# A one-core chain of three transformer blocks: the first two weight tiles after four norms taken together by TensorE

## The reference

```
hn = rmsnorm(h, norm_w)
proj = hn @ w_in
```

## Time and profile before

| what | value |
|---|---|
| median of 3 runs | 4354.56 us (4347.96 to 4360.67) |
| the profiled execution | 4353.11 us, span 4351.3 us |
| mean granted PE clock | 0.931 of full |
| PE busy | 3978.3 us, 91% |
| DVE busy | 2144.5 us, 49% |
| ACT busy | 917.8 us, 21% |
| POOL busy | 1042.5 us, 24% |
| chain that ended last, by engine | PE 82%, DVE 11%, ACT 3%, DMA 2%, issue 2%, POOL 1% |

### The profile page before, as it was taken

One profiled execution on the slowest core, in us unless ns is written; L12 is line 12 of the kernel. 1 busy time (PEld: TensorE's weight loads), 2 busy tenths in 40 slices (PEclk: granted clock), 3 DMA queues, 4 the chain that ended last, 5 costly groups with the idle time before them and its releaser, 6 DMA issues.

```text
span 4351.3 us, 49214 instructions
## 1 busy us (share of the span) xinstructions
PE 3978.3 (91%) x19946; PEld 3238.7 (74%) x19946; DVE 2144.5 (49%) x2770; ACT 917.8 (21%) x1652; POOL 1042.5 (24%) x581
## 2 busy tenths in 40 slices
PE   7899998999999999999898996799989698889898
PEld 6677676788888888788776684677778577777777
DVE  3454546332333344999334433443335984753554
ACT  2434334200000032111011001302211112531031
POOL 1120220334434422333211120021222231003221
PEclk9999999999999998999999997797999897879999
DMA  1000000111121110222211111020473134212111
GB/s 74 25 30 16 30 30 16 63 63 58 64 66 58 63 34 30 83 87 82 73 41 47 49 55 66 25 72 20 134 109 79 58 103 131 66 51 77 63 44 58
DMA packets 139196, 260.31 MB, mean 60 GB/s; under 512 B 45584, under 2 KB 87568, under 8 KB 135952
## 3 DMA queue, kind: packets, MB, share of 16 engines
q1 hardware_dynamic: 72208, 156.26, 12.3%
q10 hardware_dynamic: 66816, 101.63, 6.9%
HBM read 209.35 MB, written 46.14 MB: 59 GB/s over the span
## 4 chain that ended last, share of the span: by engine, by line
PE 82%; DVE 11%; ACT 3%; DMA 2%; issue 2%; POOL 1%; ACTq 0%; SPq 0%; DVEq 0%; POOLq 0%
PE bank L543 22%; PE bank L544 21%; PE bank L545 21%; PE bank L650 4%; PE bank L779 2%; PE bank L912 2%; PE bank L742 1%; PE bank L1041 1%; PE bank L901 1%; PE bank L762 1%; DVE hn L1738 1%; DVE fb L1876 1%; DVE xl L1749 1%; DVE s5t L2206 1%; DVE pb L2205 1%
## 5 line engine op out<-in xcount | busy, mean ns | idle before, releaser
L543 PE MATMUL bank<-xh,wh 128*128 128x512 f32 x3008 | 1201.2, 399 | 118.8 <-ACT xc L1550 39.1
L544 PE MATMUL bank<-xl,wh 128*128 128x512 f32 x3008 | 1183.8, 394 | 0.0
L545 PE MATMUL bank<-xh,wl 128*128 128x512 f32 x3008 | 1182.4, 393 | 0.0
L500 POOL CAST wh<-raw 128x1024 fp32r<-128x1024 f32 x264 | 282.9, 1072 | 3196.7 <-PE bank L545 3142.6
L543 PEld LDWEIGHTS bank<-xh,wh 128*128 128x128 f32 x3008 | 573.1, 191 | 280.0 <-issue 85.4
L502 POOL TENSOR_TENSOR wl<-raw,wh 128x1024 fp32r<-128x1024 f32 x264 | 673.0, 2549 | 21.1
L545 PEld LDWEIGHTS bank<-xh,wl 128*128 128x128 f32 x3008 | 572.2, 190 | 122.2
L544 PEld LDWEIGHTS bank<-xl,wh 128*128 128x128 f32 x3008 | 573.3, 191 | 114.1
L2015 DVE SCALAR_TENSOR_TENSOR bank<-apad,cols,bank 128x512 f32<-128x512 f32 x406 | 267.9, 746 | 0.0
L1785 DVE TENSOR_TENSOR h<-bank,h 128x512 f32<-128x512 f32 x240 | 165.9, 691 | 183.9 <-PE bank L545 183.1
L1876 DVE TENSOR_TENSOR_SCAN fb<-fb 128x256 f32<-128x256 f32 (+7 forms) x128 | 186.4, 1497 | 106.3 <-ACT ab L1228 106.3
(11 more groups left out here) (331 smaller groups left out, 5488.1 us busy)
## 6 DMA issues: line engine op xcount, KB each, us to landing
raw<-in_wstream SPq DMA_DIRECT2D x264, 512.0 KB, 3.5
spills<-spill ACTq DMA_DIRECT2D x40, 512.0 KB, 2.7
rawm<-in_mod_w ACTq DMA_DIRECT2D x12, 1024.0 KB, 4.9
gate_spill<-gates ACTq DMA_DIRECT2D x16, 512.0 KB, 2.6
tabs<-in_rope ACTq DMA_DIRECT2D x4, 2048.0 KB, 8.2
f<-spills SPq DMA_DIRECT2D x8, 1024.0 KB, 5.8
h<-in_x ACTq DMA_DIRECT2D x4, 1024.0 KB, 11.9
tabs<-gate_spill ACTq DMA_DIRECT2D x4, 1024.0 KB, 7.2
```

The source lines that it names most:

```text
L500: nc.gpsimd.tensor_copy(wh[:, slot], raw[:, slot]).then_inc(S("panel_high"), 1)
L543: nc.tensor.matmul(o, lh, rh, start=start, stop=False)
L544: nc.tensor.matmul(o, lh, rl, start=False, stop=False)
L545: return nc.tensor.matmul(o, ll, rh, start=False, stop=stop)
```

## The change

PE takes the first two tiles after each of the four norms together in a new function `first_pair`: in each half, step s multiplies feature tile s for tile 0 into bank 0 and feature tile s-2 for tile 1 into bank 1. The units are renumbered: 0 and 1 are the first half of tile 0 and of tile 1, 2 and 3 the second half (before: 0 and 1 were the two halves of tile 0). The engines that take them out go by the new numbers; their places in the lists of ACT and DVE behind the norm stay. The first two panels' slots are free after 3 and 4 units in place of 2 and 4.

```diff
+PAIR_LAG = 2
+FIRST_FREED = [3, 4]
+
+
+def pair_unit(m, th, paired=True):
+
+    return 2 * th + m if paired else 2 * m + th
...
     start = [key for name in ("q0", "k0", "v0") for key in project(name)]
+    start[:4] = [start[n] for n in (0, 2, 1, 3)]
+    unit_of.update({key: n for n, key in enumerate(start)})
+    freed[:2] = FIRST_FREED
...
-                    split(panels(name, i) + m, before[m] if m < 2 else units(name, i) + PANEL_UNITS[name][m - 2])
+                    split(panels(name, i) + m, before[m] if m < 2 else units(name, i) + freed_after(name, i, m - 2))
...
+            def freed_after(name, i, m):
+
+                if i is None and m < 2 and name in ("ffn_first", "conv", "s5_u"):
+                    return FIRST_FREED[m]
+                return PANEL_UNITS[name][m]
...
-                        turn(name, i, [units(name, i) + (PANEL_UNITS[name][dp - 2 + m] - UNITS[name])
+                        last = None if i == 1 else i - 1
+                        turn(name, i, [units(name, i) + (freed_after(name, last, dp - 2 + m) - UNITS[name])
                                        for m in range(2)])
...
+            def first_pair(unit, panel, norm):
+
+                split_done(panel + 1)
+                slots = [(panel.b + m) % 2 for m in range(2)]
+                for th in range(2):
+                    t = slice(th * HALF, (th + 1) * HALF)
+                    for step in range(KT + PAIR_LAG):
+                        if step < KT:
+                            pe.wait_ge(S("norm_low"), SPLIT0[norm] + th * KT + step + 1)
+                        for m in range(2):
+                            k = step - PAIR_LAG * m
+                            if not 0 <= k < KT:
+                                continue
+                            if k == 0:
+                                bank_free(unit + pair_unit(m, th))
+                            mm = mm3(banks[m][:, :], wh[:, slots[m], k, :], wl[:, slots[m], k, :], xh[:, k, t],
+                                     xl[:, k, t], k == 0, k == KT - 1)
+                            if k == KT - 1:
+                                mm.then_inc(S("unit_done"), 1)
 
...
-                        if key[:2] == ("q", 0):
-                            pe.wait_ge(S("norm_low"), SPLIT0["mix"] + u * KT + k + 1)
...
+            first_pair(units("attn"), panels("attn"), "mix")
+            for key in ATTN_START[4:]:
...
                 def hidden(unit, panel, split=None):
-                    for m in range(4):
-                        tile_x(unit + 2 * m, panel + m, split=split if m == 0 else None)
+                    if split is not None:
+                        first_pair(unit, panel, split)
+                    for m in range(2 if split is not None else 0, 4):
+                        tile_x(unit + 2 * m, panel + m)
...
+            def plain(name, split=None, paired=False):
                 for i in turns(pe, TURNS[name]):
+                    if paired and isinstance(i, int):
+                        first_pair(units(name), panels(name), split)
+                        continue
...
                 for i in turns(pe, KT):
-                    for m in range(4):
-                        tile_x(units("conv", i) + 2 * m, panels("conv", i) + m,
-                               split="first_final" if isinstance(i, int) and m == 0 else None)
+                    if isinstance(i, int):
+                        first_pair(units("conv"), panels("conv"), "first_final")
+                    for m in range(2 if isinstance(i, int) else 0, 4):
+                        tile_x(units("conv", i) + 2 * m, panels("conv", i) + m)
...
-                    A(qT[:, i % 2, u * HALF:(u + 1) * HALF], banks[u][:, :], ACT.Copy, scale=HEAD_DIM ** -0.5
-                      ).then_inc(S(f"bank_free{u}"), 1)
+                    b = a_unit(key).b % 2
+                    A(qT[:, i % 2, u * HALF:(u + 1) * HALF], banks[b][:, :], ACT.Copy, scale=HEAD_DIM ** -0.5
+                      ).then_inc(S(f"bank_free{b}"), 1)
...
-                def hidden(unit, gh_before, parity):
+                def hidden(unit, gh_before, parity, first=False):
                     for m in range(2):
+                        paired = first and m == 0
                         for th in range(2):
-
-                            produced(act, unit + (4 * m + th))
-                            A(sa[:, th, :], banks[th][:, :], ACT.Silu).then_inc(S(f"bank_free{th}"), 1)
+                            u = unit + (4 * m + pair_unit(0, th, paired))
+                            produced(act, u)
+                            A(sa[:, th, :], banks[u.b % 2][:, :], ACT.Silu).then_inc(S(f"bank_free{u.b % 2}"), 1)
                         for th in range(2):
-                            evicted(act, unit + (4 * m + 2 + th))
+                            evicted(act, unit + (4 * m + pair_unit(1, th, paired)))
                             A(gh[:, parity, m, th * HALF:(th + 1) * HALF], gt[:, th, :], ACT.Copy
                               ).then_inc(S("gh_ready"), 1)
...
+                order = [(j, th) for j in range(2) for th in range(2)]
+                for j, th in order if n else sorted(order, key=lambda x: x[1]):
+                    u = unit + pair_unit(j, th, n == 0)
+                    produced(act, u)
+                    if n >= 2:
+                        act.wait_ge(S("conv_in"), 2 * (n - 2) + th + 1)
+                    A(sv[:, n % 2, j, th * HALF:(th + 1) * HALF], banks[u.b % 2][:, :], (ACT.Sigmoid, ACT.Copy)[j]
+                      ).then_inc(S(f"bank_free{u.b % 2}"), 1)
...
                 for i in turns(act, 4):
                     n = i
                     unit = units(name, None if isinstance(i, int) else i)
+                    together = paired and isinstance(i, int)
+                    if together:
+                        for u in range(4):
+                            spill_tile(unit, u % 2, u // 2, u, func, permuted)
                     for m in range(2):
                         before = first // 2 + n if isinstance(n, int) else n + first // 2
                         if not (isinstance(n, int) and before == 0):
                             act.wait_ge(S(f"spilled{m}"), before * 16)
+                        if not together:
+                            for th in range(2):
+                                spill_tile(unit, m, th, 2 * m + th, func, permuted)
                         for th in range(2):
-                            produced(act, unit + (2 * m + th))
-                            o, b = spill[:, m, th * HALF:(th + 1) * HALF], banks[th][:, :]
-                            if permuted:
-                                q = S5_BLOCKS // 2
-                                o = spill[:, m, :].rearrange("p (t b) -> p b t", t=S5_TAU)[:, th * q:(th + 1) * q, :]
-                                b = b.rearrange("p (b t) -> p b t", t=S5_TAU)
...
-                    V.tensor_copy(kT[:, i % 2, u * HALF:(u + 1) * HALF], banks[u][:, :]
-                                  ).then_inc(S(f"bank_free{u}"), 1)
+                    b = a_unit(key).b % 2
+                    V.tensor_copy(kT[:, i % 2, u * HALF:(u + 1) * HALF], banks[b][:, :]
+                                  ).then_inc(S(f"bank_free{b}"), 1)
...
-                def hidden(unit, gh_before, parity):
+                def hidden(unit, gh_before, parity, first=False):
                     for m in range(2):
+                        paired = first and m == 0
                         for th in range(2):
-                            evicted(dve, unit + (4 * m + th))
-                            produced(dve, unit + (4 * m + 2 + th))
+                            evicted(dve, unit + (4 * m + pair_unit(0, th, paired)))
+                            u = unit + (4 * m + pair_unit(1, th, paired))
+                            produced(dve, u)
                             if m or unit.i is not None:
                                 dve.wait_ge(S("gl_ready"), gh_before + (2 * m + th - 1))
-                            V.tensor_tensor(gt[:, th, :], sa[:, th, :], banks[th][:, :], ALU.mult
-                                            ).then_inc(S(f"bank_free{th}"), 1)
+                            V.tensor_tensor(gt[:, th, :], sa[:, th, :], banks[u.b % 2][:, :], ALU.mult
+                                            ).then_inc(S(f"bank_free{u.b % 2}"), 1)
```

More of the change, by code:

```diff
@@ L782, in values @@
                 mm.then_inc(S("value_done"), 1)
-            for key in ATTN_START:
+            first_pair(units("attn"), panels("attn"), "mix")
+            for key in ATTN_START[4:]:
                 attn_project(key)
@@ L841, in side_product @@
                          [(ph[:, t, :], pl[:, t, :]) for t in range(2)])
-            def plain(name, split=None):
+            def plain(name, split=None, paired=False):
                 for i in turns(pe, TURNS[name]):
+                    if paired and isinstance(i, int):
+                        first_pair(units(name), panels(name), split)
```

(35 more changed lines are left out.)

## The result

The changed kernel takes 4379.12 us (median of 4 runs, 4374.42 to 4381.78). The kernel before took 4353.39 beside it (4 runs, 4347.96 to 4360.67). The ratio is 1.0057, with an interval of 1.0039 to 1.0075: slower by 25.7 us. The forecast was 4379.0 and "slower". The profiled execution took 4380.88 us, its span 4379.1; the mean granted clock went from 0.931 to 0.925.

A forecast was written before the change was run, and what follows sets the result against it. PE, 91% busy, was taken to bound the kernel. Delays of 3.1 ("ffn"), 4.2 ("conv"), 3.9 ("s5_u") and 13.2 us ("mix") sum to 24.4 on the profiled 4353.11, giving a median of 4379.0; range 4366 to 4386.

The forecast's parts named there:

- No bank comes free before ACT's sixteenth high part: After all four norms: both banks stay full until then, so the second half starts where unit 2 started before.
- the pairing pays: Rival: banks come free during the splitting; 5 us less at three norms, 16 in "mix", 31 in all; chance 0.04.
- What the change saves is nothing: All four norms: two units gained early are paid back by two left over; saving nothing.
- Cold restart: PE restarts at half clock after idling some 8 us between the pair's halves: 2.5 us lost each, range 0 to 2.7.
- v0 at 103.1: In "mix": PE waits for DVE's k0 eviction, then two panel splits in a row; v0 at 103.1, not 89.84, +13.2 us.
- The third panel: After the pair: its slot frees only after unit 2, so the third tile starts at T + 15.2 us, T being the restart.
- Rule and row: At the four restarts: the skill's rule gives full clock, the trace row 0.50 after a 7.96 us gap; forecast followed the row.
- v0's delay is covered: Rival, "mix": something else holds the attention's first steps as long, 13.2 us drop out, +11.2 us, 4365.8; chance 0.06.
- More is late: Rival: later fourth panels also catch PE, or the clock stays low longer; some 10 us more, 4389; chance 0.03.

The follow-up runs named there:

- Experiment 4: The changed kernel with the pair's second halves in free banks 4 and 7, so they wait for no eviction: 4345.79 us, ratio 0.998.
- experiment 6: The changed kernel with four banks for the pair, k0 taken out by ACT, and the modulation's halves split one place later on POOL: 4326.69 us, ratio 0.9931.
- experiment 3: The changed kernel with PE kept busy in the waits by matmuls into a spare bank that nobody reads: 4370.26 us, ratio 1.003.
- experiment 1: The changed kernel with the pairing undone after the norm "mix", the other three norms still paired: 4367.32 us, ratio 1.003.

## Why the prediction was right

**The main step held.** "No bank comes free before ACT's sixteenth high part" decides the case. Experiment 4 gives the pair free banks and nothing else, and the pair turns from +25.7 us to -10.2, with stage gains of 6.5 and 5.1 us where the rival "the pairing pays" had 5 each. In "mix" the same rival had 16 us, and 14.1 (experiment 6) needed k0 taken out by ACT and not by DVE as well. So the rival's prices were about right (31 us in all, for 33.5 by the rows of experiment 6 and 27.2 by its medians), and its condition was what the diff didn't meet.

**"What the change saves is nothing"** held: the restarts stand at the distances from the sixteenth high part that were forecast (3.78 us in "ffn" for 3.79, 2.78 for 2.76 in "conv", 1.72 for 1.77 in "s5_u").

**The terms, one by one.** The sum was 24.4 us, the rows give 21.2: the main terms were too large.
- Cold restart, 2.5 us each: experiment 3 measured 1.6 to 2.1. How long the low clock lasts is not the same each time: behind the 7.96 us gap 12 matmuls were slow, behind the one that ends at 85.30 the chain shows a pace of 0.43 us up to the seventh, 0.34 for the eighth and 0.23 from the ninth. The 2.5 us were the price of twelve slow matmuls, and the four restarts that count here had eight to ten.
- v0 at 103.1: it came at 101.09. DVE reached k0 at 84.56, not 85.74. Before, L1813 took 1.47 us beside POOL's first split, and now, with that split moved to 94.16, the same operation (L1870) takes 0.19. A step moved out of DVE's way gave something back, which the sum had at nothing. POOL also began 8.9 us after the restart and not 9.7.
- The third panel held: a wait of 1.7 us ("the pair itself would be over at T + 13.5", the tile at T + 15.2): measured 1.63 to 1.71.
- Three slips that changed nothing: tile 1 joins after nine matmuls of the second half, not six; the low end of the range is 4375 less 6.6, so 4368 and not 4370; and the first of v0's two splits was hidden before by PE's own wait for q0, not by work. v0's own slow start was in no term, and is there on both sides.

**The median agreed better than its parts.** The forecast missed by 0.1 us, and that is luck: the 3.2 us too much in the stages were made good by drift between them. The measured steps carry it to about 3 us, not closer.

**Rule and row.** The row was right about the restart. The Trainium skill, TensorE: Matmul & The Clock Gate, section "Loop structure matters more than you think", says that the copy out of PSUM between tiles doesn't break PE's warmth; here the waits of 6.4 to 13.7 us for such a copy each end in a clock of 0.50. Experiment 3 shows that it is the standing still: with matmuls in the gap and 1.3 to 2.1 us of idling left, all five restarts in the pairs ran at a clock of 1.00. The section's condition, that the next matmuls follow at once, is the point.

**The other rivals.** "v0's delay is covered" fell with experiment 1 (11.3 us by the rows, 14 by the medians, come back when "mix" is undone). "More is late" fell: PE has no wait at the fourth tile of "ffn", "conv" or "s5_u".

## What to carry to other kernels

Before two tiles are interleaved, count the banks that they need at once, and look in the list of the engine that empties each bank for what stands ahead of that eviction. It is not the eviction's 0.6 us that counts but its place: the same pairing cost 25.7 us with two banks, gained 10.2 with four, and 27 to 29 with four and the lists of ACT, DVE and POOL in order. Look first for a gain that needs no restructuring: taking the first two tiles out ahead of ACT's small functions was worth 12.3 us in the kernel before.

## What the hardware showed that was not expected

**DVE stands while POOL works on the same memory.** Small operations of DVE that take 0.18 or 0.19 us took 0.84 to 2.22 beside POOL's splits, and ended with POOL's instruction. The kernel before has it as well, in DVE's order of time and POOL's:
```profile
66.67 1.47 DVE L1813 TENSOR_TENSOR s5c<-s5c 128x32 f32<-128x32 f32 x1 [3.19 <-ACT s5c L1193]
```
```profile
65.76 2.34 POOL L502 TENSOR_TENSOR wl<-raw,wh 128x1024 fp32r<-128x1024 f32 x1
```
66.67 + 1.47 = 68.14 and 65.76 + 2.34 = 68.10. After the change, with POOL idle there, the same operation:
```profile
66.77 0.19 DVE L1870 TENSOR_TENSOR s5c<-s5c 128x32 f32<-128x32 f32 x1 [3.19 <-ACT s5c L1237]
```
POOL's own TENSOR_TENSOR took 2.34 us with DVE idle (98.69 after the change), and 2.34 to 2.41 in the rows with DVE's small operations beside it. The Trainium skill, SBUF — State Buffer, section "Who interferes with whom", says that DVE and GpSimd share one pair of SBUF ports; that an instruction of DVE with two inputs in SBUF contends there with one of GpSimd that reads SBUF, and so does one in DVE's two-port modes, which copies and tensor_scalar can enter; and that in these modes whoever issues first holds the pair for its whole instruction. These rows agree, down to the ends of the instructions; which mode DVE was in no row shows. It means that an earlier POOL can be a later ACT: in experiment 4 the wait went from POOL to DVE's constants, and from them to ACT's eviction of q0, 4.4 us late.
